# Finer order and two more PSUM banks in the mixer of a two-layer hybrid decoder on 8 cores

## The reference

```python
for l in range(2):
    h = rms_norm(x, norm1_g[l])
    u_a, v_a, val_b, gate_b = split(h @ w_in[l])        # 512 columns each
    u = gelu(u_a); v = layer_norm(gelu(v_a))
    a = u * (tril(w_s[h]) @_positions v + b_s[h])       # chunks of 128 positions, 4 heads
    g = val_b * sigmoid(gate_b)
    c = causal_depthwise_conv(g, width=31) + conv_b
    c = silu(layer_norm_in_4_groups_of_128_channels(c))
    x = x + concat([a, c]) @ w_out[l]
    h = rms_norm(x, norm2_g[l])
    x = x + relu(h @ w_ff1[l])**2 @ w_ff2[l]
out = rms_norm(x, final_g)
```

## Time and profile before

| what | value |
|---|---|
| median of 14 runs | 3224.54 us (3220.32 to 3607.09) |
| the profiled execution | 3224.97 us, span of its slowest core 3223.8 us |
| spans of the 8 cores | 3213.3 to 3223.8 us |
| busy shares | PE 93%, DVE 51%, ACT 30%, POOL 15% |
| granted TensorE clock | 0.978 to 0.981 of full speed |
| DMA | 222.59 MB a core, mean 69 GB/s |

### The profile page before, as it was taken

One profiled execution on the slowest core, in us unless ns is written; L12 is line 12 of the kernel. 1 busy time (PEld: TensorE's weight loads), 2 busy tenths in 40 slices (PEclk: granted clock), 3 DMA queues, 4 the chain that ended last, 5 costly groups with the idle time before them and its releaser, 6 DMA issues.

```text
span 3223.8 us, 42710 instructions; the slowest of 8 cores (3213.3 to 3223.8 us)
## 1 busy us (share of the span) xinstructions
PE 3004.7 (93%) x13890; PEld 1381.6 (43%) x13890; DVE 1644.3 (51%) x2513; ACT 969.2 (30%) x1549; POOL 478.5 (15%) x894
## 2 busy tenths in 40 slices
PE   4899998999899999899988999989998899989998
PEld 1444444444344444444434444444443444444443
DVE  3743466534574346643456533754446643475444
ACT  2251134312434113422144312342124422134212
POOL 5000050001400005000130001400022000140000
PEclk9999999999899999999989999999999999999999
DMA  6365506553356530745426453165531745326431
GB/s 126 53 88 75 74 1 88 70 79 55 103 70 88 76 56 1 105 62 75 75 77 88 70 79 53 15 90 79 76 82 53 101 65 75 49 33 84 67 53 53
DMA packets 201065, 222.59 MB, mean 69 GB/s; under 512 B 4113, under 2 KB 184337, under 8 KB 200722
## 3 DMA queue, kind: packets, MB, share of 16 engines
q0 software_dynamic: 183040, 184.56, 41.5%
q1 hardware_dynamic: 17810, 35.30, 3.6%
HBM read 387.61 MB, written 16.78 MB: 125 GB/s over the span
## 4 chain that ended last, share of the span: by engine, by line
PE 75%; DVE 11%; issue 7%; ACT 3%; DMA 2%; SPq 1%; DVEq 0%; ACTq 0%
PE ps L107 75%; DVE F L107 3%; DVE H L107 2%; DMA X<-xT 2%; DVE RT L107 2%; DVE VN L107 1%; DVE MIX L107 1%; ACT U L107 1%; DVE ST L107 1%; SPq L107 1%; DVE X L107 1%; ACT SIG L107 1%; ACT L107 1%; ACT F L107 1%; DVEq L104 0%
## 5 line engine op out<-in xcount | busy, mean ns | idle before, releaser
L107 PE MATMUL ps<-H,W 128*128 128x512 bf16 x5632 | 1250.4, 382 | 57.9 <-DVE GLU L107 33.2
L107 PE MATMUL ps<-F,W 128*128 128x512 bf16 x4096 | 898.9, 381 | 6.7 <-DVE F L107 6.7
L107 PEld LDWEIGHTS ps<-H,W 128*128 128x128 bf16 x5632 | 552.1, 98 | 741.9 <-issue 99.4
L107 DVE TENSOR_TENSOR X<-ps,X 128x512 f32<-128x512 f32 x640 | 439.8, 690 | 589.8 <-PE ps L107 589.8
L107 PEld LDWEIGHTS ps<-F,W 128*128 128x128 bf16 x4096 | 401.9, 98 | 496.6 <-issue 20.8
L107 ACT ACTIVATE SIG<-ps 128x512 f32<-128x512 f32 x320 | 191.2, 597 | 1255.9 <-PE ps L107 1227.5
L107 POOL TENSOR_SCALAR W<-CM,PV 128x128 bf16<-128x128 f32 x704 | 320.2, 456 | 357.8 <-PE ps L107 245.3
L260 POOL DMA_DIRECT2D W<-w_ff x128 | 112.1, 876 | 1623.6 <-PE ps L107 1623.6
L107 DVE TENSOR_TENSOR F<-ps,SIG 128x512 bf16<-128x512 f32 x256 | 176.8, 691 | 301.7 <-ACT SIG L107 301.7
L107 PE MATMUL ps<-GLU,W 128*128 128x512 bf16 x1408 | 314.9, 379 | 4.3 <-DVE MIX L107 4.3
L107 DVE SCALAR_TENSOR_TENSOR RT<-GLU,PV,RT 128x512 f32<-128x512 bf16 x448 | 309.5, 747 | 0.0
(11 more groups left out here) (52 smaller groups left out, 1181.8 us busy)
## 6 DMA issues: line engine op xcount, KB each, us to landing
W<-w_ff POOLq DMA_DIRECT2D x128, 1024.0 KB, 11.5
W<-w_in POOLq DMA_DIRECT2D x32, 1024.0 KB, 10.9
X<-xT SPq DMA_DIRECT2D x64, 256.0 KB, 7.6
W<-w_out POOLq DMA_DIRECT2D x16, 1024.0 KB, 15.0
outT<-MIX SPq DMA_DIRECT2D x16, 1024.0 KB, 4.4
PV<-pv SPq DMA_DIRECT2D x1, 1692.0 KB
BIASR<-sb SPq DMA_DIRECT2D x1, 4.0 KB
```

What stands on the lines that cost most here:

```text
L107: ins = fn()
```

## The change

`next_bank` rotates over six banks in place of four. `conv_var` and `conv_epi2` are replaced by `conv_s2`, which does one channel group: the variance matmul into bank 6 or 7, then Ln, Exp and the DVE product at once. `merge` can weight the steps of its first list, and two merges of the mixer use it: in `a1` a GLU step counts 2, a V or U step 1 and `win_vln` 0.3; in the merge with `ch1` an sgu step counts 1.4, a `conv_mm` 5.52 and a `conv_s2` 0.3. The first half's SiLU is emitted before the second group of the second half's conv, not after it.

```diff
     def next_bank():
         b = _bank[0]
-        _bank[0] = (b + 1) % 4
+        _bank[0] = (b + 1) % 6
         return b
...
-    def merge(a, b):
+    def merge(a, b, wa=None):
         na, nb = len(a), len(b)
+        wa = [1.0] * na if wa is None else list(wa)
+        tot = float(sum(wa)) or 1.0
         ia = ib = 0
+        ca = 0.0
         while ia < na or ib < nb:
-            if ib >= nb or (ia < na and ia * nb <= ib * na):
+            if ib >= nb or (ia < na and ca * nb <= ib * tot):
                 a[ia]()
+                ca += wa[ia]
                 ia += 1
             else:
                 b[ib]()
...
-    def conv_var(gi):
-        mm_group(4 + gi, [(ONESB[:], SQ[:, gi, :], ["ONESB", ("SQ", gi)])])
-
-    def conv_epi2(tt):
-        for gi in range(4):
-            sd_ap, sdk = SD2(gi)
-            P.op("act", partial(nc.scalar.activation, out=sd_ap, in_=PS[4 + gi][:], func=AF.Ln,
-                                bias=EPSC[:], scale=1.0 / 128.0),
-                 reads=[("PS", 4 + gi), "EPSC"], writes=sdk)
...
+    def conv_s2(tt, gi):
+        vb = 6 + gi % 2
+        mm_group(vb, [(ONESB[:], SQ[:, gi, :], ["ONESB", ("SQ", gi)])])
+        sd_ap, sdk = SD2(gi)
+        cc_ap, cck = CCS2(tt, gi)
+        P.op("act", partial(nc.scalar.activation, out=sd_ap, in_=PS[vb][:], func=AF.Ln, bias=EPSC[:], scale=1.0 / 128.0),
+             reads=[("PS", vb), "EPSC"], writes=sdk)
+        P.op("act", partial(nc.scalar.activation, out=sd_ap, in_=sd_ap, func=AF.Exp, scale=-0.5), reads=sdk, writes=sdk)
+        P.op("dve", partial(nc.vector.tensor_tensor, out=cc_ap, in0=cc_ap, in1=sd_ap, op=ALU.mult),
+             reads=cck + sdk, writes=cck)
...
-            merge(a1, ch0[n_u:])
+            merge(a1, ch0[n_u:], wa=[2.0] * 4 + [1.0] * 4 + [0.3] + [1.0] * 4)
...
-            cv = [partial(conv_mm, l, 0, 0, fids),
-                  partial(conv_mm, l, 0, 1, fids), partial(conv_var, 0),
-                  partial(conv_mm, l, 0, 2, fids), partial(conv_var, 1),
-                  partial(conv_mm, l, 0, 3, fids), partial(conv_var, 2)]
-            merge(sgu_steps(l, 0) + sgu_steps(l, 1) + cv, ch1)
-            conv_mm(l, 1, 0, fids); conv_var(3)
-            conv_epi2(0)
-            conv_mm(l, 1, 1, fids)
+            c_mm = (KW - KD + 1) * 0.24
+            cv = [(partial(conv_mm, l, 0, 0, fids), c_mm),
+                  (partial(conv_mm, l, 0, 1, fids), c_mm), (partial(conv_s2, 0, 0), 0.3),
+                  (partial(conv_mm, l, 0, 2, fids), c_mm), (partial(conv_s2, 0, 1), 0.3),
+                  (partial(conv_mm, l, 0, 3, fids), c_mm), (partial(conv_s2, 0, 2), 0.3)]
+            sg = [(st_, 1.4) for st_ in sgu_steps(l, 0) + sgu_steps(l, 1)]
+            allp = sg + cv
+            merge([x_[0] for x_ in allp], ch1, wa=[x_[1] for x_ in allp])
+            conv_mm(l, 1, 0, fids); conv_s2(0, 3)
             conv_silu(l, 0)
-            conv_var(0)
-            conv_mm(l, 1, 2, fids); conv_var(1)
-            conv_mm(l, 1, 3, fids); conv_var(2); conv_var(3)
+            conv_mm(l, 1, 1, fids); conv_s2(1, 0)
+            conv_mm(l, 1, 2, fids); conv_s2(1, 1)
+            conv_mm(l, 1, 3, fids); conv_s2(1, 2); conv_s2(1, 3)
             for gi in range(4):
                 ring.release(fids[("tap", gi)])
-            conv_epi2(1)
             w0 = wout_steps(l, 0, fids)
             run(w0[:4])
             conv_silu(l, 1)
```

## The result

The changed kernel takes 3143.3 us in the median (lowest 3138.4); the ratio to the kernel before is 0.9747, 95% interval 0.9734 to 0.9759, so some 82 us or 2.5% less. The forecast was 3144.5.

A forecast was written before the change was run, and what follows sets the result against it. PE, busy 93%, was taken to bound the kernel, with 219 us outside its busy time to win from. Gains of 68 + 7.2 + 6.0 - 3 + 2.3 = 80.5 us took 3225 to 3144.5 us, range 3136 to 3176.

The forecast's parts named there:

- The sgu stage: Between U and the conv, eight passes: earlier MIX products and six banks start the conv 8.5 us earlier, 68 us.
- the open price: Sgu stage: whether the clock stays up after the remaining 1.4 us wait; no loss taken, at worst 25 us.
- the first rival: Low clock in every sgu stage, 3.1 us a pass, 25 us over eight: 3170 us, chance 0.17.
- GLU in the second layer: Pass start, four passes: six banks remove the 1.79 us wait for GLU's product, 7.2 us.
- the 6.0 there: GLU, first pass: third step fills 3.5 us of the wait, and the clock staying up saves 2.5 us.
- Block starts: GLU at the start of blocks 2 to 4: between 0.8 us won and 2.2 lost each, taken as -3 us.
- The worse end: Block starts: the low clock falls on the fourth GLU step, which loses 2.2 us each.
- The output projection: Fifth group's 0.28 us wait for a bank, behind DVE's late X additions, goes with six banks: 2.3 us.
- conv_s2: nothing: Conv's variance and normalisation: PE's matmul order and the operation counts stay, so conv_s2 gains no time.
- the slower rival: A conv_s2 product waits on DVE, delaying conv steps PE needs: 3235 us or more, chance 0.02.
- The rival that DVE gets no lead: Moved conv steps delay GLU's products, first MIX product stays at 506.98: 21 us less gain, 3166 us, chance 0.10.
- the last rival: Sgu steps wait for VN or Gelu, not banks; only 15 us of other parts: 3210 us, chance 0.03.

The follow-up runs named there:

- a1's weights alone: Changed kernel with an even merge of the sgu stage, six banks and conv_s2 kept: first 3154.1 and 3179.1 us, second time 3154.7 us, ratio 0.9786.
- the run with four banks: Changed kernel with four banks and both merges even, conv_s2 and the earlier SiLU kept: 3216.6 us, ratio 0.9985 to the kernel before.
- more of DVE's work earlier: Changed kernel with 12 instead of 7 conv steps of the first half merged with U: 3130.8 us, ratio 0.9719 to the kernel before.

## Why the prediction was right

- **The sgu stage** was 68 us of 80.5 forecast, and is 8.5 us a pass, 68 in all. Its two causes were rightly told apart: banks without weights wait 4.3 us before the seventh step, weights without banks 3.4 before the fifth. In both of these runs the clock fell, so their times alone would not have told the causes apart.
- **The clock** was the open price. On the slowest core the stage stayed at 1.00 in all eight passes after waits of 1.64 us, and over all cores it fell in 7 of 64. So "no loss" was nearly right, but it had one row of another stage behind it, and some luck: with a1's weights alone, where two waits of under 0.8 us follow that of 1.64, the clock fell in 23 of 64. The price itself is real: after 3.0 to 4.3 us the clock fell in nearly every pass of the experiments. But it is smaller than the 3.1 us a pass of the first rival, 0.8 to 2.2 with five banks. The Trainium skill (TensorE: Matmul & The Clock Gate, section "What's actually happening") has the throttled state as the default that activity releases; here a wait of 1.64 us brought it back in 7 cases of 64, one of 4.29 in all 64.
- **GLU in the second layer**: 7.2 forecast, 7.7 measured by weight loads; eight waits became one of 1.8 us. That one is in the first pass, where 0.7 had been expected to be left, so the 6.0 there are some 5.
- **Block starts**: -3 us forecast as a mean between the ends (+0.8 and -2.2 have their middle at -0.7 each, not at -1). The worse end was right in its sum, but not in its parts. PE waits 6.9 us for the squares of X, the clock falls to 0.68 on the mean, and the fourth GLU step begins in it: it takes 4.5 to 5.3 us in place of 3.4. That is less than the 3 us of the worse end, but the step also starts 0.1 to 2.1 us later than before, where I had it 0.8 earlier. From the first GLU matmul to U, by weight loads, the passes lose 3.1, 1.7 and 2.1 us, 7 in all. The row of the worse end alone, 6.50 us for 16 matmuls after a wait of 6.46, would have given -6.6.
- **The output projection**: 2.3 us forecast, 3.5 measured, as 0.44 us in each pass; the step named the wrong part. Six banks were to remove the wait; the run with four banks removed it too, as conv_s2 lets DVE begin its additions 3.4 us earlier. So the step that failed is "conv_s2: nothing": it was wrong by these 3.5 us, and the banks, put at 2.3 here, are left without a gain of their own beside it.
- **conv_s2 in the queues**: no product on DVE holds back a partial sum that PE needs; from the conv's first weight load to the output projection's PE takes 43.0 us in both traces, and the slower rival has no trace.
- The rival that DVE gets no lead falls with the DVE rows: the first MIX product comes 486.00 - 477.20 = 8.8 us after U's end, not 506.98 - 495.53 = 11.5. The forecast had 504.30 - 495.53 = 8.8.
- **The sum.** The terms as measured give 68 + 7.7 + 5 - 7 + 3.5 = 77 us, not 80.5, and the two spans differ by 80.7. The missing 3.5 lie where the forecast had nothing: 4.7 won at the program's start and in V of the first passes of blocks, 1.2 lost in the MLP, all of it less than the cores of one run differ in these stretches. So the main term was foreseen, and that the total agrees to some 1 us is luck. A slip without weight: the last rival counts 15 us for the other parts, which add up to 12.5.

conv_s2 has a second use that was only argued: with the old form, which holds banks 4 to 7 until four variances are read, the rotation could not have been widened to six without meeting them in banks 4 and 5. That form with six banks wasn't tried.

## What to carry to other kernels

A wait of the busiest engine for a bank has two cures, more banks and a shorter queue on the engine that frees them; count how many groups back a bank was last used, and replay the freeing engine's queue by the rows. Weigh the steps of a merge by the time that they give the other engine, since an even count leaves that engine idle in one stage and late in the next. When a wait is gone, look at once at what the queue holds next: here it was a load behind output transfers, worth 47 us against the 82 of the whole change.

## What the runs showed of the hardware

The clock answers to short waits in this stage, and not always in the same way. Counted over eight cores with eight passes each, from the first sgu matmul to the conv's start:

| longest wait in the stage | run | passes in which the clock fell |
|---|---|---|
| 0.8 us | more of DVE's work earlier | 0 of 64 |
| 1.64 us | the changed kernel | 7 of 64 |
| 1.64 us, then two under 0.8 | a1's weights alone, second time | 23 of 64 |
| 2.97 us | five banks | 56 of 64 |
| 3.4 us | the weights without the banks | 63 of 64 |
| 4.29 us | the banks without the weights | 64 of 64 |

From 1.64 to 3.4 us the same wait goes either way, and what decides is not shown. Both cases of five banks, the second and the fifth pass, with the same wait ahead of them:

```profile
core 4: us, PE busy (x) PEld busy (x) DVE busy (x) ACT busy (x) POOL busy (x), PEclk, DMA share, GB/s
493.60:500.00 6.40, 6.37 (x33) 5.82 (x34) 6.40 (x12) 0.00 (x0) 0.00 (x0) 0.54 1.10 145
1692.20:1698.60 6.40, 5.88 (x44) 4.63 (x45) 6.40 (x12) 0.00 (x0) 0.00 (x0) 1.00 1.12 162
```

So a wait of this stage can cost it half the clock as well, and taking the wait away can then gain more than the wait itself: 8.5 us a pass here, where the waits fell from 0.72 + 6.07 + 0.54 = 7.3 to 1.6 us. The other surprise is the landing time in SP's queue: a load lands in 7.8 us in the median behind output transfers and in 4.3 us ahead of them, and the output transfers trade places with it, 4.3 and 7.4 us.
